# Five modulation chunks of layer 1 as row products on VectorE, and the attention's division on ScalarE

## The reference

```
def ada_modulation(cond, w, b):
    m = jax.nn.silu(cond) @ w + b            # cond: 1024, w: 1024 x 6144
    m = m.reshape(cond.shape[0], 1, N_MOD, D_MODEL)
    return tuple(m[:, :, i] for i in range(N_MOD))

def modulate(x, g, shift, scale):
    return rms_norm(x, g) * (1.0 + scale) + shift

# per layer: x = x + g1 * mixer(modulate(x, ...)); x = x + g2 * experts(modulate(x, ...))
# attention: p = softmax(q k^T / 8); o = p v; m = o @ w_o
```

## Time and profile before

| | |
|---|---|
| median of 3 runs | 763.27 us (761.48 to 763.44) |
| the profiled execution, its own time | 759.59 us |
| its span | 757.5 us |
| TensorE busy | 647.5 us (85%) |
| VectorE busy | 297.0 us (39%) |
| ScalarE busy | 133.1 us (18%) |
| moved by DMA | 291.12 MB, 384 GB/s over the span |

### The profile page before, as it was taken

How to read it: one execution, slowest core, us unless ns; L and a number is a source line. 1 busy time by engine, 2 the same in 40 slices (tenths; PEclk the granted TensorE clock), 3 DMA queues, 4 the chain that set the end, 5 groups by cost and what they waited for, 6 DMA issues and landing times.

```text
span 757.5 us, 12788 instructions
## 1 busy us (share of the span) xinstructions
PE 647.5 (85%) x4711; PEld 349.6 (46%) x4711; DVE 297.0 (39%) x724; ACT 133.1 (18%) x330; POOL 120.6 (16%) x194
## 2 busy tenths in 40 slices
PE   4999999999999999999745678899999997564586
PEld 3533343436795755554322333647655553222242
DVE  2114618674315544444311113666544443112123
ACT  5002234553127200000000000654000000000000
POOL 1000000001000133333211001010343333111110
PEclk9999999999999999999966689999999999677799
DMA  9999959959089699999999999999999999999997
GB/s 330 422 430 427 415 235 391 399 220 418 31 333 387 263 395 424 416 420 416 422 424 420 424 420 376 416 427 418 374 419 408 421 422 417 420 422 422 423 419 291
DMA packets 40009, 291.12 MB, mean 384 GB/s; under 512 B 7514, under 2 KB 8946, under 8 KB 20496
## 3 DMA queue, kind: packets, MB, share of 16 engines
q1 hardware_dynamic: 30544, 272.46, 87.0%
q0 software_dynamic: 7600, 12.81, 4.8%
q10 hardware_dynamic: 1808, 5.06, 1.7%
HBM read 284.68 MB, written 17.56 MB: 399 GB/s over the span
## 4 chain that ended last, share of the span: by engine, by line
PE 63%; DMA 25%; DVE 4%; SPq 4%; issue 2%; ACT 1%; DVEq 0%; POOLq 0%; POOL 0%
PE bank L1804 17%; DMA ring<-in_moe_w_in 9%; PE bank L1490 8%; PE bank L1841 8%; PE bank L1400 5%; DMA cond_at<-in_moe_w_in 4%; DMA ring<-in_moe_w_out 4%; PE bank L1604 4%; DMA adas<-in_moe_w_in 3%; PE bank L1763 2%; PE bank L1612 2%; DMA adaw<-rows,gidx 2%; PE bank L1543 2%; PE bank L1564 2%; PE bank L1708 2%
## 5 line engine op out<-in xcount | busy, mean ns | idle before, releaser
L1804 PE MATMUL bank<-ring,qkv 128*32 128x256 f32 (+1 forms) x1344 | 135.5, 428 | 38.5 <-DMA ring<-in_moe_w_in 25.8
L1804 PEld LDWEIGHTS bank<-ring,qkv 128*32 128x32 f32 (+1 forms) x1344 | 77.4, 134 | 82.3 <-issue 52.5
L1232 DVE COPY qkv<-bank 128x512 f32<-128x512 f32 x44 | 30.4, 692 | 200.7 <-PE bank L1763 200.7
L607 POOL DMA_INDIRECT results<-adaw,scur x46 | 47.2, 1027 | 249.8 <-DVE adaw L1255 218.0
L883 ACT ACTIVATE qkv<-bank 128x128 f32<-128x128 f32 x48 | 13.3, 278 | 408.4 <-PE bank L1804 408.4
L1841 PE MATMUL bank<-ring,qkv 128*32 128x512 f32 (+1 forms) x368 | 65.7, 601 | 1.4 <-DMA ring<-in_moe_w_out 1.4
L1490 PE MATMUL bank<-ring,hT 128*128 128x512 f32 x144 | 64.6, 599 | 1.8 <-DVE hT L973 1.8
L1804 PE MATMUL bank<-seventh,qkv 128*64 128x256 f32 (+1 forms) x224 | 35.4, 483 | 16.7 <-DMA ring<-in_moe_w_in 16.7
L597 POOL DMA_INDIRECT adaw<-rows,gcur x40 | 41.6, 1040 | 33.0 <-POOL gcur L594 27.7
L1490 PEld LDWEIGHTS bank<-ring,hT 128*128 128x128 f32 x144 | 26.5, 190 | 37.9 <-issue 35.2
L1804 PE MATMUL bank<-xT,qkv 128*64 128x256 f32 (+1 forms) x192 | 30.8, 486 | 14.4 <-DMA cond_at<-in_moe_w_in 14.4
(11 more groups left out here) (266 smaller groups left out, 837.0 us busy)
## 6 DMA issues: line engine op xcount, KB each, us to landing
ring<-in_moe_w_in SPq DMA_DIRECT2D x37, 2048.0 KB, 17.1
ring<-in_moe_w_out SPq DMA_DIRECT2D x44, 1024.0 KB, 26.7
ring<-in_ada_w SPq DMA_DIRECT2D x14, 2048.0 KB, 13.6
adaw<-in_ada_w SPq DMA_DIRECT2D x10, 2048.0 KB, 14.9
adaw<-in_moe_w_in SPq DMA_DIRECT2D x8, 2048.0 KB, 22.3
seventh<-in_moe_w_in SPq DMA_DIRECT2D x8, 1792.0 KB, 25.0
xT<-in_moe_w_in SPq DMA_DIRECT2D x8, 1536.0 KB, 20.2
hT<-in_moe_w_out SPq DMA_DIRECT2D x10, 1024.0 KB, 25.2
```

The lines of the kernel that those rows point to most:

```text
L607: pool.indirect_dma_start(res, bass.IndirectOffsetOnAxis(ap=scur[:, p, :], axis=0), yout[:, p], None, bounds_check=res_limit, oob_is_err=F ...
L1232: V.tensor_copy(xgT[:, p], bank[2][:, :]).then_inc(xgT_ready, 1)
L1804: last = T.matmul(bank[p][64 * a + m * h:64 * a + m * (h + 1), 0:2 * P], xk[:, k % 4, k // 4, m * h:m * (h + 1)], gate_up_of(b, k)[:, :, a ...
```

## The change

Chunks 19 to 23 (`BY_ROWS`, the last five of layer 1) leave TensorE. Their weights are laid out in memory the other way round, with a map's column on each partition and its 1024 inputs along the row. VectorE multiplies such a row block with the conditioning vector, spread over all partitions, and sums along the row (`row_product`, a `tensor_tensor_reduce`). A chunk takes four blocks times two vectors, so 8 products of 128x1024. Two loads of 512 KB (written) bring the conditioning vectors to all partitions, and ScalarE takes their SiLU. Chunk 19 is multiplied ahead of the second half of the modulation, 20 and 21 during the projection, 22 and 23 in the attention, one product in each of the steps 0 to 15. TensorE's remaining chunks get later slots. ScalarE divides the probabilities (an activation with a scale of its own per row), and VectorE only makes the reciprocal. The loads get another order and other places, and a semaphore `ada_rows` counts the chunks done on VectorE.

```
+BY_ROWS = (19, 20, 21, 22, 23)
+        ADA_LOADS = [0, 2, 19, 1, 3, 20, 21, 4, 5, 6, 7, 22, 8, 9, 10, 11, 12, 13, 14, 23, 15, 16, 17, 18]
+        ADA_AT = dict(zip(ADA_LOADS, (TAIL, LEFT, RIGHT, HIGH0, HIGH1, TAIL, LEFT, RIGHT, HIGH0, HIGH1, TAIL, LEFT,
+                                      RIGHT, HIGH0, HIGH1, TAIL, RIGHT, HIGH0, HIGH1, LEFT, TAIL, RIGHT, TAIL, RIGHT)))
-        AFTER_QKV = {g: 3 + g for g in range(1, 9)}
-        ADA_STEPS = {1: 12, 2: 13, 3: 14, 4: 15, 5: 16, 7: 17, 9: 18, 11: 19, 13: 20, 15: 21, 16: 22, 17: 23}
+        AFTER_QKV = {4: (4,), 5: (5,), 6: (6, 7), 7: (8, 9)}
+        ADA_STEPS = {u: 10 + n for n, u in enumerate((1, 2, 3, 5, 7, 9, 11, 13, 15))}
 ...
             def load_ada(i):
-                if ADA_PRIOR[i] >= 0:
-                    sp.wait_ge(ada_mm, ADA_RANK[ADA_PRIOR[i]] + 1)
+                users = ADA_USERS[ADA_AT[i]]
+                n = users.index(i)
+                if n and users[n - 1] in BY_ROWS:
+                    sp.wait_ge(ada_rows, BY_ROWS.index(users[n - 1]) + 1)
+                elif n:
+                    sp.wait_ge(ada_mm, ADA_RANK[users[n - 1]] + 1)
 ...
+            def row_product(i, b, cond):
+                w = ada_place[ADA_AT[i]].rearrange("p (b d) -> p b d", b=4)[:, b]
+                if b == 0 and cond == 0:
+                    dve.wait_ge(s_adaw[ADA_AT[i]], 16 * (ADA_USERS[ADA_AT[i]].index(i) + 1))
+                m = 4 * (i % NCH) + b
+                last = V.tensor_tensor_reduce(w if cond else row_products, w, cond_rows[:, cond], 1.0, 0.0,
+                                              ALU.mult, ALU.add, mods[:, i // NCH, m, cond:cond + 1])
+                if b == 3 and cond == 1:
+                    last.then_inc(ada_rows, 1)
+                else:
+                    order(last)
 ...
-            for g in range(2):
-                qk_stats(g)
-                qk_norm(g)
+            row_chunk(BY_ROWS[1])
+            qk_stats(0)
+            row_chunk(BY_ROWS[2])
+            qk_norm(0)
+            qk_stats(1)
+            qk_norm(1)
 ...
+                if u < 16:
+                    row_product(BY_ROWS[3 + u // 8], u % 8 // 2, u % 2)
 ...
+                if 1 <= u < NU + 1:
+                    act.wait_ge(sc_inverse, v + 1)
+                    for j in range(2):
+                        last = A.activation(probs[:, v % 4, j, 0:nk], probs[:, v % 4, j, 0:nk], ACT.Copy, scale=inverse)
+                    last.then_inc(sc_normed, 1)
```

More of the change, by code:

```diff
@@ L450, in load_qkv @@
                              attn_w_qkv[n][:, half * HALF * 512:(half + 1) * HALF * 512]).then_inc(s_wqkv[n], 16)
[L452 to L457, removed]
+            load_ada(0)
+            load_ada(2)
+            load_qkv(0, 0)
+            load_qkv(1, 0)
+            for i, v in enumerate((c_ctx.rearrange("(o d) -> o d", o=1), c)):
+                sp.dma_start(cond_rows[:, i], v[0:1, :].to_broadcast([P, D])).then_inc(s_condrows, 16)
+            load_qkv(2, 0)
+            load_ada(BY_ROWS[0])
+            load_ada(1)
+            load_ada(3)
+            load_ada(BY_ROWS[1])
+            for n in range(3):
+                load_qkv(n, 1)
+            for i in ADA_LOADS[6:]:
                 load_ada(i)
-                if ADA_AT[i] == TAIL and i > 20:
-                    sp.wait_ge(ada_mm, 20)
-                    sp.dma_start(wo.rearrange("p k n -> p (k n)"), attn_w_o).then_inc(s_wo, 16)
+            sp.wait_ge(ada_mm, max(ADA_RANK[ADA_USERS[place][-1]] for place in (HIGH0, HIGH1)) + 1)
+            sp.dma_start(wo.rearrange("p k n -> p (k n)"), attn_w_o).then_inc(s_wo, 16)
             for l in range(2):
                 if l == 0:
-                    sp.wait_ge(ada_mm, 2 * NCH)
+                    sp.wait_ge(ada_mm, BY_ROWS[0])
+                    sp.wait_ge(ada_rows, len(BY_ROWS))
                     load_out(l, 3, 3, s_wout[3])
@@ L711, in _ @@
             set_copy(0)
+            act.wait_ge(s_condrows, 32)
+            for i in range(2):
+                A.activation(cond_rows[:, i], cond_rows[:, i], ACT.Silu).then_inc(cond_ready, 1)
             set_copy(1)
@@ L960, in _ @@
                 first = half * HALF
+                if half:
+                    dve.wait_ge(cond_ready, 4)
+                    row_chunk(BY_ROWS[0])
                 dve.wait_ge(ada_vec, half + 1)
@@ L1034, in _ @@
                     v = u - 1
-                    nk = P if UNITS[v][0] == 0 else 3 * P
                     dve.wait_ge(sc_exp, v + 1)
-                    order(V.reciprocal(rt[:, 64 + 2 * (v % 4):66 + 2 * (v % 4)], rt[:, 2 * v:2 * v + 2]))
-                    for j in range(2):
-                        c = 64 + 2 * (v % 4) + j
-                        last = V.tensor_scalar(probs[:, v % 4, j, 0:nk], probs[:, v % 4, j, 0:nk], rt[:, c:c + 1], None,
-                                               ALU.mult)
-                    last.then_inc(sc_normed, 1)
+                    V.reciprocal(rt[:, 64 + 2 * (v % 4):66 + 2 * (v % 4)], rt[:, 2 * v:2 * v + 2]).then_inc(sc_inverse, 1)
                 if 2 <= u < NU + 2:
@@ L1319, in _ @@
             modulation(3, 0, 5, 6)
-            vectors_of(3, 1, 0, 6 * KD)
+            vectors_of(3, 1, 0, 4 * (BY_ROWS[0] - NCH))
+            dve.wait_ge(ada_rows, len(BY_ROWS))
+            m = mods[:, 1, 4 * (BY_ROWS[0] - NCH):, :]
+            order(V.tensor_tensor(m, m, bias[:, 1, 4 * (BY_ROWS[0] - NCH):].unsqueeze(2).to_broadcast([P, 4 * len(BY_ROWS), 2]),
+                                  ALU.add))
             V.memset(ss[:, 17:18], 0.0).then_inc(mods_ready, 1)
@@ L1509, in _ @@
                     pe.wait_ge(qkv_sq, 1)
+                for i in AFTER_QKV.get(g, ()):
+                    ada(i)
                 if g == 7:
```

48 lines of the change are left out of this document (29 added, 19 removed).

## The result

The changed kernel takes 782.93 us in the median of 4 runs (779.77 to 785.20), against 763.36 for the kernel before: a ratio of 1.0265, 95% interval 1.0242 to 1.0287. It is slower by 19.6 us in the medians. The profiled execution took 780.93 us, its span 779.1; against the profiled execution of the kernel before (759.59) that is 21.3 us more.

What follows compares the result with a forecast made beforehand. TensorE was taken to bound the kernel, with the attention's shift arriving in the total one for one. Terms -1.4, +3.5, +11.6 and +3.5 gave +17.2 us: 776.8 profiled, 780.5 on the median, 778 stated; range 764 to 794.

Steps and rivals of the forecast that it cites:

- Projection, -1.4: Layer 0's projection: two chunks fewer on TensorE, less chunk 1's late landing and a copy; attention starts 1.4 us earlier.
- A product, 1.43: One 1024-wide row product on VectorE with the read of its sum: 1.43 us, bounds 1.25 to 1.65.
- Steps 0 to 7, +3.5: Early attention: TensorE waits for ScalarE's division and copy, reaching the chunk of step 9 3.5 us later.
- The wait in step 9, +11.6: Attention: chunk 15's load, queued behind 23's, which waits for VectorE's chunk 22, makes TensorE wait 11.6 us.
- Behind it, +3.5: From chunk 15 to the output projection: half clock, two chunks fewer, VectorE and ScalarE pacing; +3.5 us, bounds 0 to +6.
- the half clock: Behind the wait in step 9, chunk 15 runs at the 1.2 GHz level: +1.85 us.
- no change: Rival: the wait in step 9 is covered, +3.8 us at most, about +1; 764 us on the median; chance 0.08.
- the rival "faster": TensorE sets every attention step, chunk 23's place free by 21 instead of 33: -7.0 us, 756 on the median; chance 0.07.

Runs made afterwards that it cites:

- e1_order: Changed kernel with chunk 23 behind 15 and 16 in SyncE's load list, every chunk keeping its place: 780.79 us, ratio 1.0225.
- e5_spread: e2_places with TensorE's nine attention chunks in steps 1, 2, 3, 4, 5, 8, 10, 12 and 16: 771.38 us, ratio 1.0110.
- e6_both: e2_places with the division of the probabilities back on VectorE instead of ScalarE: 773.10 us, ratio 1.0128.
- e2_places: Changed kernel with the same load order but other places for chunks 23, 15, 16, 17 and 18: 770.97 us, ratio 1.0100.
- e8_two: Kernel before with only chunks 22 and 23 as row products, during the projection, loaded behind the projection's own loads: 762.93 us, ratio 0.9999.
- e10_start: e8_two with chunk 10 put behind the projection's last product: 762.72 us, ratio 1.0001.
- e7_step4: e4_projection with the chunk of attention step 17 moved to step 4: 760.03 us, ratio 0.9967.
- e4_projection: Kernel before with only chunks 21 to 23 as row products, ahead of and during the projection, division still on VectorE: 762.98 us, ratio 1.0004.
- e9: e7_step4 with chunk 10 put behind the projection's last product, attention chunks moved up by one: 760.54 us, ratio 0.9978.
- e3: Kernel before with only the division of the probabilities moved to ScalarE, all chunks staying on TensorE: 765.15 us, ratio 1.0037.

## Why the prediction was right, and where its terms were off

The direction, the mechanism and its place came as forecast, and the time inside the range; 778 was 4.9 us too low. Half of that is the choice of 778: the same sum on the median gave 780.5, 2.4 too low. By the traces the sum was +21.2 instead of +17.2 at the output projection:

- **Projection, -1.4: measured -0.7.** Chunk 1 came at 41.5, as said. Not foreseen: behind a wait of 1.22 us for VectorE, which the kernel before has as well, the changed kernel's clock fell to 0.58 in 54 to 58 us, and the next 40 products took 19.1 us instead of 17.4. e1_order, e5_spread and e6_both, the same program up to there, ran these 4 us at 1.00 and started their attention at 110.5 to 110.9; e2_places, the same program too, fell to 0.73. So these 1.7 us come and go from one execution to the next, and are luck in a single trace.
- **A product, 1.43: measured 1.22 and 0.08**, 1.26 from its start to that of the next operation. The nearest row was the tensor_tensor of the same size, 1.225, and not the form with two operations; the read of the sum costs half of a reciprocal. The Trainium skill's rule (Vector Engine (DVE) Microarchitecture Reference, section Points that are easy to get wrong), half throughput for one instruction format with two SBUF sources that aren't bf16, isn't seen in these traces. The row product takes 1.22 us for 1024 elements, but the profile names it CUSTOM_DVE_ANT_0, and whether it has that format no run shows; the scalar_tensor_tensor of 512 takes 0.752 with both sources in SBUF and 0.751 with one of them in a PSUM bank.
- **Steps 0 to 7, +3.5: measured +4.4** (chunk 15's turn at 147.90, 35.8 behind the first scores). Step 5 waits 3.36, 3.45 was said. I had missed 1.16 us in step 2 for the first exponentials, since chunk 11 no longer stands ahead of the scores. The clock fell behind step 5's wait too: transposes and scores take 1.11, 0.63 and 1.65 instead of 0.66, 0.38 and 0.92. That cost nothing. The value product of step 6 waits for ScalarE's copy anyway, and it starts 3.9 us behind those transposes here (133.17 to 137.06) and in e2_places (133.10 to 137.00), where the transposes run at full clock.
- **The wait in step 9, +11.6: measured +12.4.** Chunk 22 ends 33.7 behind the first scores (33.1 said), and the second chunk is there 14.1 behind its issue (13.3 said): the first of the two took 9.6 instead of 8.4, the second 4.9 more, as said.
- **Behind it, +3.5: measured +5.0.** Chunk 15 at half clock costs 1.7 (1.85 said). The short steps 16 and 17 leave TensorE waiting 1.04 and 1.13 and the clock falls again: from the transposes of step 17 to the output projection it takes 8.17 us (191.86 to 200.03), against 5.94 in e5_spread at full clock (178.27 to 184.21), so 2.2 more.

The 40 products of the projection in the changed kernel, then in e1_order:

```profile
54.53 19.10 PE L1544 MATMUL bank<-ring,hT 128*128 128x512 f32 x40 [1.22 <-DVE hT L1024]
```

```profile
54.61 17.41 PE L1544 MATMUL bank<-ring,hT 128*128 128x512 f32 x40 [1.22 <-DVE hT L1024]
```

The mechanism was right; the term that was mis-sized is the half clock. I took it once, behind the longest wait. It came three times more, behind waits of 1 to 3.4 us, and cost TensorE twice: 1.7 us in the projection and 2.2 at the end, 3.9 of the 4.0 by which the sum was short. That the rest comes out even is luck: the wait of step 2 (1.16) and the later landing (0.8) were missing, and the other terms were some 2 us too high.

One sentence on the rivals was wrong. I wrote that there would be no change if SyncE could pass 15 ahead of 23. e1_order does that and saves 2 to 3 us at most: VectorE's wait for 23 isn't "inside of" TensorE's, it is the next one in line. And e2_places meets the second condition of the rival "faster", 23's place free early, and is still 1% slower: the first, that VectorE and ScalarE stay under TensorE's steps, isn't met.

The attention's shift arrived in the total for the 21 and the 9 us of the first kernels. For 2 or 3 us the total isn't as good a witness: e8_two and e10_start show a loss elsewhere, and e7_step4's median gained more (2.8 us) than its traced output projection (0.7).

## What to carry to other kernels

When a load waits for a buffer that a slower engine gives back, price the wait of every user behind it, not of the nearest one alone: putting the queue in another order only hands the wait on, and another place for the data takes it away. Work moved to an idle engine is nearly free in the stretches where that engine idles, as long as its loads delay nobody (two chunks of 1.85 us brought 3.5 us at the first scores in e8_two, but two brought only 0.6 in e4_projection, where chunk 1 came late and the clock fell). It costs in the stretches where the idle engine comes to set the step, as here in the attention; there, fill the busy engine's steps where the other is late, as the chunk in step 4 does. Give every wait of more than a microsecond on TensorE the chance of a half clock behind it, and ask whether the next wait hides it, as in step 6 of the changed kernel.

## What the runs showed of the hardware

- The granted clock fell behind waits of TensorE of only 1.2 us in some executions and not in others: 0.58, 0.73, 0.63, 0.60 and 0.67 in 54 to 58 us (the changed kernel, e2, e4, e7, e9) against 1.00 (the kernel before, e1, e3, e5, e6, e8, e10), behind 1.22 each (1.28 in e8 and e10). The changed kernel, e1, e2, e5 and e6 are one program up to there, so the program alone doesn't decide it. The wait for chunk 1, some 13 us earlier, was 0.80 to 1.37 us in the five with the fall, and 1.50 to 1.82 or none in the others; whether that matters isn't shown.
- In the changed kernel the clock was down at 192 to 196 with TensorE busy in all 4 us: the level belongs to what came before, here two waits of about 1 us within 3.5 us. e2_places, with the same two waits (1.04 and 1.13), fell to 0.77 in 180 to 184; e5_spread, with 1.04 and 0.68, stayed at 1.00.
- A multiplication with a sum along the row of 128x1024 costs what the one without a sum costs (1.220 against 1.225 us), and the read of the sum 0.08.
- Two tensor_scalar of 128x384 on VectorE took 2.36 us instead of 0.75 in a step where a memset on GpSimd ran beside them (e6_both); that it is the reason isn't shown.
- A stall of 2 us that the profile puts down to no event stood in the traces of e8_two and e10_start and in none of the other ten. With one trace of each, it isn't shown whether it belongs to the program or to the execution.
